# Block 0's last norm moved from before the last V pass into its second quarter, and four pairs of late rows put at weight positions 1 to 4

## The reference, cut to what matters

```
u_sel = jnp.take(peer_u, ib, axis=0)
act = jax.nn.gelu(jnp.einsum('thkd,td->thk', u_sel, xb), approximate=False) * gb
v_sel = jnp.take(peer_v, ib, axis=0)
return jnp.einsum('thk,thkd->td', act, v_sel)
...
x = layer_norm(DN_ALPHA * x + y_ffn, ln3_g[l], ln3_b[l])
```

## Time and profile before

| | us |
|---|---|
| median of three runs | 3251.5 |
| the profiled execution's own time | 3250.64 |
| its span in the trace | 3248.8 |
| PE busy | 3093.9 (95%) |
| DVE busy | 2076.6 (64%) |
| POOL busy | 680.0 (21%) |
| ACT busy | 363.7 (11%) |
| HBM read, mean rate | 1007.08 MB, 316 GB/s |

### The profile page before, as it was taken

The page is one execution under the profiler, slowest core; times in us unless marked ns, Lnnn a source line. Parts: engine busy times, 40 slices in busy tenths (PEclk is TensorE's granted clock), DMA queues, the critical chain, the costliest instruction groups (busy, mean ns, idle before and its releaser), DMA issues.

```text
span 3248.8 us, 26700 instructions
## 1 busy us (share of the span) xinstructions
PE 3093.9 (95%) x10342; PEld 1894.5 (58%) x10342; DVE 2076.6 (64%) x2878; ACT 363.7 (11%) x650; POOL 680.0 (21%) x551
## 2 busy tenths in 40 slices
PE   8999999999999889999989999999999989999697
PEld 5444444444445677788854448874368844478443
DVE  5355543432778689879976766655665666556675
ACT  1223212401001211112210000000000000000000
POOL 0000000000212233322213232222222233223230
PEclk9999999999999999999999999999999999999899
DMA  7222221187996679989989999999999999999985
GB/s 271 78 73 76 81 71 46 38 303 251 361 402 246 265 325 389 421 321 355 347 303 391 389 422 421 418 418 416 421 421 421 418 418 416 421 422 419 407 366 229
DMA packets 152518, 1029.73 MB, mean 317 GB/s; under 512 B 16464, under 2 KB 21712, under 8 KB 35664
## 3 DMA queue, kind: packets, MB, share of 16 engines
q0 software_dynamic: 78512, 557.88, 42.2%
q1 hardware_dynamic: 73888, 470.24, 37.0%
HBM read 1007.08 MB, written 20.97 MB: 316 GB/s over the span
## 4 chain that ended last, share of the span: by engine, by line
DMA 39%; PE 38%; DVE 17%; issue 3%; POOL 1%; ACT 1%; DVEq 0%; SPq 0%; ACTq 0%; POOLq 0%
DMA arena<-peer_v,arena 37%; PE ps L692 11%; DVE arena L1826 6%; PE ps L1103 5%; PE ps L1076 4%; PE ps L864 3%; PE ps L882 3%; PE ps L954 3%; DVE arena L1864 2%; DVE arena L1815 2%; PE ps L763 1%; DVE arena L1866 1%; ACT arena L1143 1%; PE ps L656 1%; PE ps L817 1%
## 5 line engine op out<-in xcount | busy, mean ns | idle before, releaser
L1103 PE MATMUL ps<-arena 128*128 128x512 f32 x2048 | 889.8, 597 | 63.1 <-DVE arena L1876 56.0
L1076 PE MATMUL ps<-arena 128*128 128x256 f32 x4096 | 894.4, 380 | 4.3 <-ACT arena L1368 3.8
L1076 PEld LDWEIGHTS ps<-arena 128*128 128x128 f32 x4096 | 777.2, 191 | 111.5 <-ACT arena L1368 4.3
L1826 DVE SCALAR_TENSOR_TENSOR arena<-arena 128x2048 f32<-128x2048 f32 x256 | 601.9, 2351 | 304.2 <-DMA arena<-peer_v,arena 231.8
L1815 DVE CUSTOM_DVE_ANT_0 arena<-arena 128x2048 f32<-128x2048 f32 x256 | 586.2, 2290 | 282.3 <-DMA arena<-peer_u,arena 280.0
L1103 PEld LDWEIGHTS ps<-arena 128*128 128x128 f32 x2048 | 392.7, 192 | 558.0 <-issue 498.2
L613 POOL DMA_INDIRECT arena<-peer_u,arena x256 | 340.3, 1329 | 1084.9 <-DVE arena L1815 894.4
L624 POOL DMA_INDIRECT arena<-peer_v,arena x256 | 317.4, 1240 | 779.9 <-DVE arena L1826 747.8
L692 PE MATMUL ps<-arena 128*128 128x512 f32 x800 | 345.2, 593 | 1.0 <-ACT arena L1143 1.0
L692 PEld LDWEIGHTS ps<-arena 128*128 128x128 f32 x800 | 152.2, 190 | 191.8 <-issue 191.8
L1143 ACT ACTIVATE arena<-ps 128x512 f32<-128x512 f32 (+2 forms) x247 | 145.6, 611 | 749.5 <-PE ps L874 143.5
(11 more groups left out here) (181 smaller groups left out, 1782.3 us busy)
## 6 DMA issues: line engine op xcount, KB each, us to landing
arena<-peer_ut SPq DMA_DIRECT2D x128, 1024.0 KB, 9.2
arena<-peer_vt SPq DMA_DIRECT2D x128, 1024.0 KB, 9.1
arena<-w_row SPq DMA_DIRECT2D x52, 1024.0 KB, 7.8
arena<-w_mix SPq DMA_DIRECT2D x48, 1024.0 KB, 5.0
arena<-w_once SPq DMA_DIRECT2D x74, 512.0 KB, 3.5
arena<-w_feat SPq DMA_DIRECT2D x20, 1024.0 KB, 9.9
dense_gates<-arena SPq DMA_DIRECT2D x8, 2048.0 KB, 7.4
arena<-dense_gates POOLq DMA_DIRECT2D x11, 1024.0 KB, 24.2
```

Source lines behind the costliest of these rows:

```text
L1076: last = pe.matmul(ps[:, (e // 2) % 4, (e % 2) * DT:(e % 2 + 1) * DT], w[:, kt * P:(kt + 1) * P], XTD[:, kt * DT:(kt + 1) * DT], start=(kt ...
L1103: last = pe.matmul(bank(4 + (c % 2) * 2 + tb), G[:, t * DT + tb * P:t * DT + (tb + 1) * P], w[:, i * 512:(i + 1) * 512], start=(t == 0), s ...
L1826: dve.scalar_tensor_tensor(out=acc, in0=VB[e], scalar=AV[r // 4 % 2][:, r % 4:r % 4 + 1], in1=acc, op0=ALU.mult, op1=ALU.add).then_inc(v_f ...
```

## The change

Block 0's norm leaves its place after position 191 and now stands in group 3 between quarter 0 and quarter 1 of the V pass, ahead of position 198. `half_pos` puts the pairs 34 to 37 at positions 1 to 4 and spreads the other 90 from position 5 on over 208 positions.

```diff
@@ -112,7 +112,8 @@
 
 def half_pos(k):
 
-    return 3 + (k - HALVES_BEFORE) * (POSITIONS - 6) // (2 * RSTEPS - HALVES_BEFORE)
+    n = k - HALVES_BEFORE
+    return 1 + n if n < 4 else 5 + (n - 4) * (POSITIONS - 8) // (2 * RSTEPS - HALVES_BEFORE - 4)
 
@@ -2004,6 +2005,10 @@
             for g in range(4):
                 first = FIRST[g] // 8
                 for c in QUAD:
+                    if g == 3 and c == 1:
+                        dve.wait_ge(gain3_in, 32)
+                        dve.wait_ge(v_free, HK)
+                        norm(ACC, ACC, GAIN3_G, GAIN3_B, dve_tick).then_inc(y_ready, 1)
                     for l in range(TILES[g] // ET):
                         if c == 0:
                             for i in range(TILES[g] // 8):
@@ -2025,10 +2030,6 @@
                                 weigh(FIRST[g + 1] // 8 + i, i)
                         rows_until(p)
                         p += 1
-                    if g == 2:
-                        dve.wait_ge(gain3_in, 32)
-                        dve.wait_ge(v_free, HK)
-                        norm(ACC, ACC, GAIN3_G, GAIN3_B, dve_tick).then_inc(y_ready, 1)
                 if g == 3:
                     link(last)
```

## The result

The changed kernel takes 3231.6 us (median of nine runs, 3225.3 to 3237.1) beside 3247.2 us of the kernel before (nine runs, 3241.0 to 3251.6) on the same chip: a ratio of 0.995, 95% interval 0.9938 to 0.9962, 15.6 us less. A second series of the two gave 0.9947 (0.9932 to 0.9962). The prediction was 3229 us, a gain of 22 us, in a range of 3220 to 3243: the direction and the range held. The drop is 0.4 to 0.6% by the interval. One execution in all series, of the kernel from position 0, took 3308.6 us at a lower granted clock and is left out.

The account below looks back on a forecast made before the run. Bytes were taken to bound DVE's rows from V0 on, with the last `weigh` setting the end. 3250.6 - 10.4 (norm) - 12.0 (early pairs) = 3228.2, with 0.9 for the median 3229 us; range 3220 to 3243.

Parts of the forecast that it names:

- What bounds the kernel: From V0 on bytes limit DVE's rows; the last `weigh` in V3, where PE waits 30.22 us, sets the end.
- Its cover in V3: At its new place the norm is covered by DVE's idle time between late transfers: 0 us, without cover 10.4.
- The four early pairs: At the start of V0 they fill idle DMA time during waits for gate tables: 12 us, ends 0 and 18.
- Nothing later can take the gain back as long as PE is still waiting at the last `weigh`: After V0 the early gain stays, since all transfers ahead of the last `weigh` are the same; PE waits 9 us there.
- the extra pair ahead of a `weigh` in V2: At position 136, one more pair costs 10 us against 12 us filled: that `weigh` comes 2 us sooner.
- signs named as right: V0 share over 0.9, norm without PE waiting, last `weigh` near 3065, PE's wait near 9 us, V2 wait 10 to 15.
- 155 us: In V3, the time from the start of the last `weigh` to the end, said to be again this long.
- signs named as wrong: Over 5 us for `add_dense` in V3's quarter 3; last `weigh` near 3077; or PE's wait there gone, its weights limiting.
- the third: Sign of being wrong: PE's wait at the last `weigh` is gone and PE's own 216 weights limit the whole.
- Only the norm pays: Rival: the four pairs bring nothing, the filled time being lost in later full buffers: 3241 us, chance 0.18.
- The tables come late: Rival at V0's start: tables 3 and 4 load beside gathers, losing about half of 12 us: 3235 us, chance 0.10.
- The wait in V3: Rival: PE waits 8 us at quarter 3's first matmul, for `add_dense` at position 204: 3237 us, chance 0.07.

Follow-up runs that it names:

- kernel from position 0: Changed kernel with pairs moved from 187 to 189 and 189 to 192, rows inside the routing work, and early pairs at positions 0 to 3: 3220.7 us.
- norm alone: Changed kernel with the old pair formula, so only block 0's norm is moved: 3237.4 us, ratio 0.9966.
- a quarter later: Block 0's norm behind quarter 1's sum, in the changed kernel with two pairs late, rows inside the routing work and tables 3 and 4 sooner: 3218.5 us.
- one pair behind 188: Changed kernel with the pair of position 187 put at 188, behind that `weigh`: 3230.7 us, ratio 0.9947.
- two early pairs: Changed kernel with two early pairs, at positions 1 and 2, instead of four: 3229.1 us, ratio 0.9934.
- the pairs alone: Kernel before with the new pair formula, the norm left at its old place: 3237.0 us, ratio 0.9971.
- rows inside the keys: Changed kernel with two pairs moved back (187 to 189, 189 to 192), and row pairs between best keys and best pairs at positions 8 and 15: 3220.5 us.

## Why the prediction was right, and where it was not

**What bounds the kernel: right.** PE's waits in V3 were set by DVE's order and that by bytes. The norm alone gave 10.7 us for a forecast of 10.4 (7 to 15 by its interval). Its cover in V3 was real: 10.4 us of DVE's time lie beside PE's matmuls without a gap, and a quarter later makes no difference.

**The four early pairs: the mechanism right, the size of the term too large.** The term was 12 us, from a share that was to rise from 0.75 to over 0.9. It rose to 0.85 to 0.87, from 0.72 and 0.77 in the two profiles of the old order, which is 5 to 9 us by share. With the last `weigh` again the place where PE waits, and 85 pairs ahead of it, it starts at 1397.3 (one pair behind 188) and 1395.6 (two early pairs). Before, the norm began there at 1406.2, and with the norm alone the `weigh` is at 1400.5: the pairs bring 9 to 11 us against the one profile and 3 to 5 against the other. By the medians they are worth 11.1 us alone (5.5 to 13 by the interval) and 5 to 6 on top of the norm. I had subtracted only 2 us for the time up to the first early pair. The engines' share was 0.34 in the first 10 us and POOL's first gather came at 1682.4, 9 us after the first `weigh`, since POOL waits until the `peer_v` row ahead of it in the order has been used.

**"Nothing later can take the gain back as long as PE is still waiting at the last `weigh`": its condition did not hold.** PE was not waiting there. I had costed the extra pair ahead of a `weigh` in V2 and not the one at position 188, where there was one more as well (84 against 83), and PE stopped two weights sooner. In the kernel with the pairs alone this covers a part of the norm at its old place (PE waits 6.68 us behind it and not 10.4). It is not what kept the changed kernel above the forecast: in the two kernels without the wait at 188 the end is at 1539.6 and 1537.4, beside 1537.4 and 1538.1.

**The number, in part luck.** Counted from the first `weigh`, the forecast put the end at 1558.6 - 22.4 = 1536.2, and it came at 1537.4, 21.2 us sooner than before. But a few us of this can lie in the one profile before: the norm alone, with the same order, is 6.9 us sooner at 188. The last `weigh` started at 3064.99 as forecast because several things met: it came 14.3 us sooner after V0's start than the norm had begun before, and not 12, while V0 began 2.2 us later. Of the signs named as right, that one and the norm without a wait beside it came. The share over 0.9, the wait of 9 us at the last `weigh` (12.22 at the one before it) and a wait of 10 to 15 us in V2 (8.44) did not. The "155 us" from the last `weigh` to the end come from no row: it was 3248.8 - 3087.51 = 161.3 us before and is 164.8 now. None of the signs named as wrong came whole; of the third, PE's wait at the last `weigh` is gone, but PE's own weights don't limit the whole.

**The rivals.** "Only the norm pays" is out: the pairs alone gave 11.1 us. "The tables come late" had its cause right and its price wrong: table 3 landed late and DVE waited 13.27 us, but the engines were busy all through that wait. The wait in V3 behind the norm, at quarter 3, didn't come in the changed kernel; in the four kernels that have a pair fewer ahead of the last `weigh` and the norm at this place it was 1.4 to 5.8 us. The waits of 4.3 to 6.2 us at quarter 2 are for the sum ahead of the norm. PE's new early waits in V0, 4.4 and 3.8 us, were followed by a shorter one in V2 (8.44 instead of 14.90), as forecast. The kernel wasn't slower; the mechanism named for that (rows of V3 short of bytes, ahead of `add_dense`) exists, at a quarter of the price of 22.7 us or less.

**What stays open.** The change's interval is 12 to 20 us, so 2 or 3 us of the account can't be checked by medians. Whether the two parts really give less together than apart is not shown, nor which share of the 12 us the pairs bring on top of the norm. Why rows inside the keys moved the end by 7.3 us where the share explains 4 is not settled; one profile each varies by that much (0.72 and 0.77 for the same stretch in the kernel before and with the norm alone, and 6.9 us at the `weigh` at 188).

## What to carry to other kernels

Where one stream (weights for the dense part) runs ahead of another (rows) on the same transfers, look for the stretches in which the transfers stand idle, and put the work of the late stream there; here two of the four early pairs were enough, a table issued sooner filled some more, and a further such place, beside the routing work, gave 3 us by the medians, which their intervals don't confirm. When a piece is taken away ahead of a wait, cost the wait before it as well, with the work that now stands ahead of that one. Two such gains can overlap: bring each out alone before adding them. And before a few us are read from a pair of profiles, compare two profiles of the same order: here they were up to 7 us apart.

## What the runs showed of the hardware that I had not expected

A gate table of 1 MB on SP's queue landed 28.7 us after its issue at most in the changed kernel, where the longest before was 19.7. PE waited 3.2 to 9.1 us for a weight of the same queue some 42 to 48 us after the first `weigh` in every kernel with early pairs, and in neither of the two without. A burst of gathers thus goes together with a delay of a stream that had come on time; in the saturated part after V0, with one gather following on another, PE waited for no weight.

POOL's instruction for a gather took 0.94 us at 1700.86 in the changed kernel, with DVE idle, and 2.74 us at 1682.40, where DVE was in a `dot` over 128x2048 with two inputs. In the kernel before, all gathers from 1640 us on that ran with DVE all but idle took 0.93 to 0.97 us, and those that started well inside such an instruction 1.9 to 3.1. So DVE's work lengthens the issue of a gather by up to 2 us, here in the stretch where the transfers stand idle.
